# Delta rule decay arguments: cumulative gate sums spread by DMA and subtracted on VectorE, in place of a masked product on TensorE

## The reference, cut to what matters

```python
gc = jnp.cumsum(g, axis=-1)
diff = gc[..., :, None] - gc[..., None, :]
decay = jnp.exp(jnp.where(tri_incl, diff, -jnp.inf))
lower = jnp.where(tri_strict, jnp.einsum('bhncd,bhnsd->bhncs', k_beta, k) * decay, 0.0)
rhs = jnp.concatenate([v_beta, k_beta * jnp.exp(gc)[..., None]], axis=-1)
sol = lax.linalg.triangular_solve(eye + lower, rhs, left_side=True, lower=True, unit_diagonal=True)
qk = jnp.einsum('bhncd,bhnsd->bhncs', q, k) * decay
```

## Time and profile before

| what | value |
|---|---|
| median of 3 runs | 2402.45 us (2402.34 to 2403.43) |
| the profiled execution's own time | 2402.18 us |
| its span in the trace | 2400.4 us |
| TensorE clock granted | 1.0 of full speed throughout |
| PE busy | 2374.3 us (99%) |
| DVE busy | 1468.1 us (61%) |
| ACT busy | 1214.0 us (51%) |
| POOL busy | 69.2 us (3%) |
| moved by DMA | 430.98 MB, mean 180 GB/s |

### The profile page before, as it was taken

One profiled execution on the slowest core, in us unless ns is written; L12 is line 12 of the kernel. 1 busy time (PEld: TensorE's weight loads), 2 busy tenths in 40 slices (PEclk: granted clock), 3 DMA queues, 4 the chain that ended last, 5 costly groups with the idle time before them and its releaser, 6 DMA issues.

```text
span 2400.4 us, 34008 instructions
## 1 busy us (share of the span) xinstructions
PE 2374.3 (99%) x11756; PEld 1973.8 (82%) x11756; DVE 1468.1 (61%) x1995; ACT 1214.0 (51%) x1858; POOL 69.2 (3%) x92
## 2 busy tenths in 40 slices
PE   8999999999999999999999999999999999999999
PEld 6888888888888888888888887878787888888887
DVE  5656555456566664466665667776766755555554
ACT  5444544444455554445454574647474554555553
POOL 0110100000100000000000000000000000000000
PEclk9999999999999999999999999999999999999999
DMA  7765565565665656665655654445454575655555
GB/s 257 224 204 165 164 184 189 180 199 186 215 193 178 189 183 198 187 199 175 185 186 185 194 152 141 142 149 150 138 149 141 176 206 176 190 164 180 174 164 170
DMA packets 286976, 430.98 MB, mean 180 GB/s; under 512 B 32656, under 2 KB 126096, under 8 KB 286736
## 3 DMA queue, kind: packets, MB, share of 16 engines
q1 hardware_dynamic: 281056, 421.12, 57.2%
q10 hardware_dynamic: 5808, 8.41, 1.0%
HBM read 427.37 MB, written 7.08 MB: 181 GB/s over the span
## 4 chain that ended last, share of the span: by engine, by line
PE 92%; DVE 3%; ACT 1%; DVEq 1%; issue 1%; DMA 1%; ACTq 0%
PE gemm L513 28%; PE gemm L515 27%; PE gemm L514 27%; PE aux L1817 2%; DVE w_lo L487 1%; PE aux L1989 1%; PE aux L515 1%; PE aux L514 1%; PE aux L513 1%; PE aux L1924 1%; ACT w_hi L477 0%; PE aux L2278 0%; DMA raw<-in_w_in 0%; PE aux L2259 0%; DVEq L1492 0%
## 5 line engine op out<-in xcount | busy, mean ns | idle before, releaser
L487 DVE TENSOR_TENSOR w_lo<-raw,w_hi 128x1024 fp32r<-128x1024 f32 (+1 forms) x800 | 959.3, 1212 | 572.9 <-ACT w_hi L477 556.0
L477 ACT ACTIVATE w_hi<-raw 128x1024 fp32r<-128x1024 f32 (+1 forms) x800 | 820.9, 1042 | 578.2 <-PE gemm L515 478.4
L513 PE MATMUL gemm<-w_lo,hT_hi 128*128 128x512 f32 x2304 | 910.6, 395 | 3.6 <-DVE w_lo L487 3.5
L515 PE MATMUL gemm<-w_hi,hT_lo 128*128 128x512 f32 x2304 | 895.4, 389 | 0.0
L514 PE MATMUL gemm<-w_hi,hT_hi 128*128 128x512 f32 x2304 | 894.4, 388 | 0.0
L513 PEld LDWEIGHTS gemm<-w_lo,hT_hi 128*128 128x128 f32 x2304 | 433.4, 188 | 93.7 <-DVE w_lo L487 6.4
L515 PEld LDWEIGHTS gemm<-w_hi,hT_lo 128*128 128x128 f32 x2304 | 432.9, 188 | 90.9
L514 PEld LDWEIGHTS gemm<-w_hi,hT_hi 128*128 128x128 f32 x2304 | 433.7, 188 | 83.5
L513 PE MATMUL gemm<-w_lo,yT_hi 128*128 128x512 f32 x472 | 184.5, 391 | 0.5 <-DVE w_lo L487 0.5
L515 PE MATMUL gemm<-w_hi,yT_lo 128*128 128x512 f32 x472 | 183.7, 389 | 0.0
L514 PE MATMUL gemm<-w_hi,yT_hi 128*128 128x512 f32 x472 | 183.7, 389 | 0.0
(11 more groups left out here) (315 smaller groups left out, 1854.8 us busy)
## 6 DMA issues: line engine op xcount, KB each, us to landing
raw<-in_w_up SPq DMA_DIRECT2D x336, 256.0 KB, 3.4
raw<-in_w_in SPq DMA_DIRECT2D x144, 512.0 KB, 4.5
raw<-in_a_w_in SPq DMA_DIRECT2D x128, 512.0 KB, 3.7
raw<-in_b_w_in SPq DMA_DIRECT2D x128, 512.0 KB, 4.2
raw<-in_w_down SPq DMA_DIRECT2D x76, 512.0 KB, 4.7
raw<-in_w_branch SPq DMA_DIRECT2D x32, 512.0 KB, 4.9
raw<-in_w_out SPq DMA_DIRECT2D x32, 512.0 KB, 4.8
raw<-in_a_w_out SPq DMA_DIRECT2D x32, 512.0 KB, 3.7
```

Of the source, the lines that this page charges most:

```text
L477: nc.scalar.activation(hi, src, ACT.Copy).then_inc(S("hi_done"), 1)
L487: nc.vector.tensor_tensor(lo, src, hi.bitcast(F32), ALU.subtract).then_inc(S("lo_done"), 1)
L513: nc.tensor.matmul(dst, xh, wl[:, k, :], start=h["start"] and k == 0, stop=False)
L515: mm = nc.tensor.matmul(dst, xl, wh[:, k, :], start=False, stop=h["stop"] and k == h["n"] - 1)
```

## The change

The 128x128 argument of the decay is no longer a product of masks and gates. The cumulative sums `gc` of all heads are kept in SBUF (`gcs`), turned once on PE to rows, written to a DRAM tensor `gc_rows` (16 KB), and read back by a DMA that gives every partition the same row (`spread_rows`, 512 KB for a group). DVE then subtracts the partition's own sum and clips at zero, one instruction for each head and row block. `dec` is then in SBUF, and one Exp covers all of it. `m_gt`, the products at L1432 and L2069 and the signal `d_gm` are gone. In `decays` the three sums on PE move one step forward and a turn takes the step behind them. `L_turned` and `products` now lie over the buffer of `o_rows`.

```diff
@@ ACT @@
+            def spread_rows(gi):
+                act.dma_start(gc_all[:, :, :].rearrange("p (t h) c -> p t (h c)", t=TB),
+                              gc_rows[:, bass.ds(gi * HG, HG), :].rearrange("t h c -> t (h c)").partition_broadcast(P)
+                              ).then_inc(S("gc_spread"), 16)
             def delta(gi):
                 yield
                 act.wait_ge(S("d_arg"), gi + 1)
-                for tb in range(TB):
-                    A(dec[:, tb * HG:(tb + 1) * HG, :], AX[2 + tb][:, :].rearrange("p (a c) -> p a c", c=P), ACT.Exp)
+                A(dec[:, :, :], dec[:, :, :], ACT.Exp)
+                if not isinstance(gi, int):
+                    spread_rows(gi + 1)
                 act.drain()
...
             def decays():
-                act.wait_ge(S("gc_done"), 1)
-                A(egc[:, :, :], AX[2][:, 0:TB * H].rearrange("p (t h) -> p t h", t=TB), ACT.Exp)
+                act.wait_ge(S("gc_out"), 1)
+                A(egc[:, :, :], gcs[:, :, :], ACT.Exp)
                 act.wait_ge(S("g_rest"), 1)
                 A(edec[:, :, :], edec[:, :, :], ACT.Exp).then_inc(S("decays"), 1)
+                act.wait_ge(S("gc_turned"), 1)
+                A(gcT[:, :], AX[3][0:TB * H, 2 * P:3 * P], ACT.Copy).then_inc(S("gc_kept"), 1)
+                act.wait_ge(S("gc_kept"), 1)
+                act.dma_start(gc_rows.rearrange("t h c -> (t h) c"), gcT[:, :]).then_inc(S("gc_written"), 16)
+                yield
+                yield
+                act.wait_ge(S("gc_written"), 16)
+                spread_rows(0)
@@ DVE, factors @@
-                dve.wait_ge(S("chunk_masks"), 1)
-                for tb in range(TB):
-                    e = V.tensor_tensor(dec[:, tb * HG:(tb + 1) * HG, :], rep(m_le[:, :], HG), each(gg[:, tb, hs], P), ALU.mult)
-                e.then_inc(S("d_gm"), 1)
@@ DVE, delta @@
             def delta(gi):
+                dve.wait_ge(S("gc_spread"), gi * 16 + 16)
+                for tb in range(TB):
+                    for h in range(HG):
+                        e = V.tensor_scalar(dec[:, tb * HG + h, :], gc_all[:, tb * HG + h, :], gcs[:, tb, bass.ds(gi * HG + h, 1)], 0.0,
+                                            ALU.subtract, ALU.min)
+                e.then_inc(S("d_arg"), 1)
                 yield
@@ DVE, decays @@
-                yield
                 dve.wait_ge(S("gc_done"), 1)
+                V.tensor_copy(gcs[:, :, :], AX[2][:, 0:TB * H].rearrange("p (t h) -> p t h", t=TB)).then_inc(S("gc_out"), 1)
@@ PE, delta @@
-                pe.wait_ge(S("chunk_masks"), 1)
-                pe.wait_ge(S("d_gm"), gi + 1)
-                for tb in range(TB):
-                    m = MM(AX[2 + tb][:, :], m_gt[:, :], dec[:, tb * HG:(tb + 1) * HG, :].rearrange("p a c -> p (a c)"),
-                           start=True, stop=True)
-                m.then_inc(S("d_arg"), 1)
                 pe.wait_ge(S("d_sums"), gi * 2 + 2)
                 gram(xk)
@@ PE, decays @@
-                for _ in range(5):
+                for _ in range(4):
                     yield
...
+                yield
+                pe.wait_ge(S("gc_out"), 1)
+                pe.wait_ge(S("g_rest"), 1)
+                turn(AX[3][0:TB * H, 2 * P:3 * P], gcs[:, :, :].rearrange("p t h -> p (t h)"), ident[:, :]).then_inc(S("gc_turned"), 1)
```

More of the change, by code:

```diff
@@ L243, in program @@
         vs = r.put("v_rows2", [P, TB, 512])
+        early = Region(r.at)
+        Lt = early.put("L_turned", [P, BASE, 2 * BASE])
+        prod = early.put("products", [P, BASE * BASE * 2])
         o_rows = r.put("o_rows", [P, TB, 512])
@@ L254, in program @@
         Um = r.put("inverse_turned", [P, TB * HG, C])
-        Lt = r.put("L_turned", [P, BASE, 2 * BASE])
         dec = r.put("decay", [P, TB * HG, P])
@@ L260, in program @@
         m_le = r.put("m_le", [P, P])
-        m_gt = r.put("m_gt", [P, P])
         idc = r.put("idc", [P, C])
@@ L275, in program @@
         Lb = r.put("L_base", [P, BASE, BASE])
-        prod = r.put("products", [P, BASE * BASE * 2])
         Zb = r.put("Z_base", [P, BASE * BASE // 4])
         Xb = r.put("X_base", [P, BASE, BASE])
+        gc_all = r.put("gc_all", [P, TB * HG, P])
+        gcs = r.put("gc", [P, TB, H])
+        gcT = r.put("gc_turned", [TB * H, P])
         W1 = [r.put(f"W1_{l}", [P, TB * HG, C]) for l in range(2)]
@@ L319, in program @@
         na_skew = nc.dram_tensor("na_bias_copies", (NAH, GRID, SKEW), F32, kind="Internal").ap()
+        gc_rows = nc.dram_tensor("gc_rows", (TB, H, P), F32, kind="Internal").ap()
         band_skew = nc.dram_tensor("band_bias_copies", (H, C, BAND), F32, kind="Internal").ap()
@@ L561, in _ @@
                 nc.gpsimd.memset(m_le[:, :], 1.0)
-                nc.gpsimd.memset(m_gt[:, :], 1.0)
                 nc.gpsimd.memset(idc[:, :], 0.0)
@@ L571, in _ @@
                     pattern=[[1, P]], channel_multiplier=-1)
-                sel(out=m_gt[:, :], in_=m_gt[:, :], compare_op=ALU.is_ge, fill=0.0, base=-1,
-                    pattern=[[-1, P]], channel_multiplier=1)
                 nc.gpsimd.memset(Xb[:, :, :].rearrange("p i j -> p (i j)")[:, 0:BASE * BASE:BASE + 1], 1.0)
```

## The result

The changed kernel takes 2418.4 us (median; 2417.89 to 2419.25) against 2402.4 in the same series: ratio 1.0065, 95% interval 1.0053 to 1.0078, 16.0 us slower. The forecast was 2410.8, range 2405 to 2417. The direction was right, the forecast rise of 8.4 us is about half of the measured one, and the time lies outside the range.

The account below looks back on a forecast made before the run. The prediction took the chain through the Exp and DVE to bound the kernel, not PE's work despite 99% busy. Group 0 +4.3, groups 1 and 2 +4.1, group 3 0: +8.4 us, 2410.8 us; range 2405 to 2417.

Parts of the forecast that it names:

- PE's 7.1 us of products: Products removed from PE over four groups of the delta rule, about 1.8 us each; gain put at nothing.
- The stall of 2.4 us: In group 0's `decays`, PE's sums, one step earlier, wait for ACT's Sigmoid (`ab_beta`); PE stands still 2.4 us.
- Group 0, +4.3 forecast: Group 0's Exp starts at 1444.7 instead of 1440.38, 4.3 us later, from PE's stall, ACT's delay and the spread's landing.
- I take 3.7, the row of this stage: Group 0's first spread: landing taken as 3.7 us, as a load of 512 KB, so it lands at 1442.8.
- the slow row of 6.3: Alternative landing of group 0's spread, from the slow broadcast row: 6.3 us, making the Exp 6.9 us later.
- Groups 1 and 2, +2.05 forecast: Inside the loop, subtractions behind the jump and a half start the Exp 2.05 us later per group, 4.1 us together.
- I take it as the price of the loop's jump on DVE: DVE's unexplained gap before the half in groups 1 and 2, 2.25 and 2.34 us, carried over as 2.3.
- estimate of 1.0 us for the eight subtractions: DVE's eight subtractions at 58 + 64 cycles each, 1.0 us; would take 1.0 us off groups 1 and 2 together.
- The signs: Expected trace: `decays` stall 2.4 us, `gram(xc)` waits about 2 a group, `w_lo` waits about 3, group 0 spread wait about 1.
- (a): Rival: PE's work is what counts, so the removed products shorten the kernel to 2395.5 us; chance 0.07.
- (d): Rival: spread landing of 8 us or more, or its issue holding ACT in three groups; 2414 to 2420 us; chance 0.12.
- (c): Rival: DVE's jump shorter or overlapping, loop groups cost 0 to 1 each, group 0 4.3; 2406 to 2408 us; chance 0.13.

Follow-up runs that it names:

- the filled stall: Twenty filler products (128x256) added on PE between its two waits of the gate sums, against the kernel after: 2418.27 us.
- The two experiments that put work ahead of the jump: Against the kernel after, ahead of DVE's loop jump: the eight subtractions of groups 1 to 3 moved there, 2409.85 us; eight useless DVE instructions added there, 2420.22 us.
- the last one: Against the version with both costs mended: subtractions of groups 1 to 3 made in place two steps sooner, beside the K convolution: 2403.86 us.

## Why the prediction was wrong

**Right in kind.** PE's 7.1 us of products gave nothing, because the chain runs through the Exp: shown by leaving them out (2.4 us over four groups, the Exp at ACT's floor) and by the waits of `gram(xc)`, which total 10.2 us. The subtractions behind the loop's jump are the cost in the loop's groups: shown by moving them ahead of it, which made groups 1 to 3 shorter by 8.9 us and the time by 8.5. The stall of 2.4 us came as worked out, and the move that causes it costs 3.8 us by itself.

**Group 0, +4.3 forecast, +9.3 measured: the step that failed.** Its working had PE go on at full rate behind the stall. In the profiled execution the clock fell to 1.2 GHz for 6.5 us, which makes 2.6 of the missing 5.0 us at the Exp (90.32 against 87.75 in the execution where it didn't fall). The other 2.4 are the landing: "I take 3.7, the row of this stage" was the row of the `raw` loads on SP's queue, and not that of a transfer on ACT's queue that shares the DMA engines with them. With the clock up, the spread was issued when the forecast had it (79.9 us behind the stage's start, forecast 79.7), so what is left is the landing of 5.9 us there. The four spreads of the kernel after landed in 5.5 to 6.4 us, near the slow row of 6.3 that the forecast kept as the far bound. 4.3 and 2.4 make 6.7, and 87.75 less 80.98 is 6.8. In whole times the clock's part is not settled: the repeated kernel's runs lie between 2415.9 and 2419.6, and the filled stall did not lower the time.

**Groups 1 and 2, +2.05 forecast, +3.30 and +3.09 measured.** The step "I take it as the price of the loop's jump on DVE" had the gap as a constant behind the last instruction. It isn't: from the start of the last short instruction of the factors to the start of the first half behind the jump it is 4.89 and 4.98 us before, with the mask product in between, and 4.24 and 4.00 after without it. So the 1.5 us that the forecast let DVE gain by the removed product came to 0.65 and 0.98, and the gap grew by the rest. The two experiments that put work ahead of the jump show the same from the other side. Another 0.2 to 0.5 is the eight subtractions: 1.75 to 2.0 us, inside the bounds given (1.1 to 2.1) and above the 1.5 taken. In group 2 a last 0.2 lies between the Exp of group 1 and the factors, and stays unexplained. Group 3's +0.90 has no jump in it: 0.5 is the subtractions (2.00 us), 0.2 the wait of the half for ACT, which the forecast hadn't, and 0.2 again lies between the Exp of group 2 and the factors.

The prediction's estimate of 1.0 us for the eight subtractions, worked out from the page "VectorE: DVE Perf Modes" of the Trainium skill (sections "The TRN2 errata" and "The perf-mode tier table"), was low as well. By the same 58 cycles the 128x256 row of 354 ns would be 194 or 327 ns, as an estimate; it lies above both and not between them, so the trace did speak against the 1.0 us.

**The signs.** The stall in `decays` (2.39 us), the wait at `gram(xc)` (10.2 us in four groups, about 2 each forecast) and the wait for the spread came. The waits for `w_lo` did not grow to about 3 us: the longest is 1.4, and there are two of them in a group instead of one.

**The rivals.** (a) is out. (d), a dearer transfer, had the right time (2414 to 2420) for a reason that covers only a part: the landing took 5.5 us and not 8, the issue held up nothing, and the clock and the jump did the rest. (c), a cheaper jump, had the mechanism that the runs show, work and jump overlapping, but on the wrong side: the overlap was already in the kernel before and hid the mask product, so that taking it out freed little. By its own terms (4.3 to 6.3 us more) its time is 2406.7 to 2408.8, not 2406 to 2408.

The page "Runtime: NRT & Kernel Launch" of the Trainium skill (section "Instruction fetch mechanics") says that a taken branch out of the fetched pages makes the engine's sequencer fetch the target before it goes on, while instructions are otherwise fetched ahead. If such a fetch starts when the sequencer reaches the branch while DVE still works on what is queued, which is an argument and not on the page, the gaps agree with it (3.24 us behind 0.75 of work, 1.88 behind 2.4). In the kernel after, the DMA view has two packets of the kind "instruction" between 1561.5 and 1565.6, but it doesn't say for which engine, so the cause of the gap is argued and not shown.

## What to carry to other kernels

Look for what a removed instruction was hiding behind: work queued ahead of a loop's jump is nearly free, so removing it saves little, and work moved behind the jump costs its full length plus the jump. When a wait on a full PE is moved, count more than the wait: here a stall of 2.4 us was followed in some executions by products at half clock. And price a new transfer by rows that fell together with another transfer, not by the median of the loads that it will compete with: that median was 3.6 us, the new transfer took 5.5, and the loads beside such transfers up to 6.6.

## What the runs showed of the hardware

- **The gap at DVE's loop jump** depends on what is queued ahead of it: 2.9 to 4.0 us behind a `tok` alone, 1.5 to 2.6 behind 2.0 to 2.4 us of work, in all fourteen profiles. From the start of the last short instruction of the factors to the first half behind the jump it is 3.9 to 5.0 us in the first case and 4.2 to 5.2 in the second. The same gap differed by up to 1 us between kernels whose code around it is equal (3.00 and 3.98 in group 2), which stays unexplained.
- **The granted clock after a short stall** isn't the same in every execution: behind PE's stall of 2.4 us it was 0.50 for 6.5 us in one profile of the kernel after and 1.00 in another, with identical instructions. Of the seven profiles with this stall unfilled (the kernel before with its sums moved is one), it fell in four. That isn't the chip alone: on one and the same chip it stayed up with the subtractions ahead of the jump and fell with the spread issued sooner. Behind PE's later waits of 1.5 to 4.4 us it likewise fell in some profiles and stayed in others: behind the 3.18 us at `gram(xc)` of group 1 in the repetition it fell, behind the 3.28 us at the same place in the first profile it didn't. The kernel before has a wait of 2.55 us and 1.00 throughout.
- **A 512 KB transfer on ACT's queue** with a source of 4 KB read 128 times landed in 4.9 to 7.2 us over nine profiles, with medians of 5.5 to 6.5, beside `raw` loads of the same size that have a median of 3.6 to 3.8. With 128 different rows as source it was 3.8 to 6.0.
- **Eight 128x128 tensor-scalar instructions** with the scalar from memory take DVE 1.65 to 2.2 us, 0.21 to 0.27 each.
- **The Exp of the decay** has a table load of 1.28 us ahead of it on ACT and starts at its end, however early its argument is: 1554.24 to 1555.54 us in the kernel with PE's products left out, 1556.90 to 1558.19 in the last one.
